# Weight requests, context products and bias products moved in a fused two-block Transformer kernel

## The reference

```
# first block: 16 experts, 32 tokens each; w_gate, w_up: 16 x 1024 x 2048, w_down: 16 x 2048 x 1024
hid = silu(xs @ w_gate) * (xs @ w_up);  eo = hid @ w_down
x = x + zeros.at[idx].add(gates * eo);  x = rms_norm(x, final_g)
# second block: context keys and values, from ctx alone
hc = modulate(rmsnorm(ctx, g_pre_mix), sh1c, sc1c)
kv_c = hc @ w_in[:, 1024:3072]          # keys 1024 columns, values 1024 columns
# second block: input projection; modulate adds the row sh1, so its product sh1 @ w_in is a bias row
h = modulate(rmsnorm(x, g_pre_mix), sh1, sc1)      # h * (1 + sc1) + sh1
q, k, v, z, gl = split(h @ w_in)                   # 7 parts of 1024 columns
```

## Time and profile before

| | us |
|---|---|
| median of 2 runs | 2217.85 (2216.74 to 2218.97) |
| the profiled execution, its own time | 2217.74 |
| its span, first to last instruction | 2215.9 |
| mean granted TensorE clock | 0.801 |
| PE busy | 1514.1 (68%) |
| DVE busy | 742.5 (34%) |
| DMA, mean over the span | 361 GB/s, 800.89 MB |

### The profile page before, as it was taken

How to read it: one execution, slowest core, us unless ns; L and a number is a source line. 1 busy time by engine, 2 the same in 40 slices (tenths; PEclk the granted TensorE clock), 3 DMA queues, 4 the chain that set the end, 5 groups by cost and what they waited for, 6 DMA issues and landing times.

```text
span 2215.9 us, 24722 instructions
## 1 busy us (share of the span) xinstructions
PE 1514.1 (68%) x10356; PEld 613.8 (28%) x10356; DVE 742.5 (34%) x1862; ACT 429.9 (19%) x998; POOL 309.4 (14%) x290
## 2 busy tenths in 40 slices
PE   9998676776565655659855988897686854434445
PEld 7554133221111111113211334454333620100001
DVE  5831100000000000000000235445767686776774
ACT  1430100000000000000000106443414542221222
POOL 0110000000000000000000000001343445444351
PEclk9999888877777777889977999898686975565555
DMA  9699989999999999999455824357999999999997
GB/s 408 269 423 383 421 348 399 402 392 428 427 429 428 428 428 427 428 420 425 197 232 232 335 88 176 114 190 293 382 418 416 421 420 420 421 421 420 421 420 308
DMA packets 76750, 800.89 MB, mean 361 GB/s; under 512 B 9088, under 2 KB 9216, under 8 KB 10592
## 3 DMA queue, kind: packets, MB, share of 16 engines
q1 hardware_dynamic: 39008, 530.66, 57.4%
q0 software_dynamic: 37632, 268.65, 29.3%
HBM read 798.03 MB, written 1.05 MB: 361 GB/s over the span
## 4 chain that ended last, share of the span: by engine, by line
DMA 42%; PE 42%; DVE 9%; ACT 3%; issue 2%; POOL 0%; SPq 0%; DVEq 0%; another core or an unknown queue 0%; ACTq 0%; POOLq 0%
DMA AR<-in_peer_uv,AR 13%; DMA AR<-in_w_up 12%; DMA AR<-in_w_down 10%; PE PS L413 5%; DMA AR<-in_w_gate 5%; PE PS L699 5%; PE PS L860 5%; PE PS L772 5%; PE PS L424 4%; PE PS L738 4%; DVE AR L1638 3%; PE PS L996 3%; PE PS L953 2%; PE PS L535 1%; PE PS L781 1%
## 5 line engine op out<-in xcount | busy, mean ns | idle before, releaser
L699 PE MATMUL PS<-AR 128*32 128x512 f32 x2048 | 330.1, 782 | 202.9 <-DMA AR<-in_w_up 129.3
L2072 POOL DMA_INDIRECT AR<-in_peer_uv,AR x256 | 293.6, 1147 | 1071.8 <-DVE AR L1629 772.7
L996 PE MATMUL PS<-AR 32*32 32x512 f32 x4032 | 224.7, 907 | 288.5 <-ACT AR L2008 285.2
L1638 DVE CUSTOM_DVE_ANT_0 AR<-AR 128x1024 f32<-128x1024 f32 x256 | 309.2, 1222 | 158.8 <-DMA AR<-in_peer_uv,AR 158.2
L738 PE MATMUL PS<-AR 128*32 128x512 f32 x1024 | 177.9, 756 | 131.4 <-DMA AR<-in_w_down 130.8
L1292 DVE TENSOR_TENSOR AR<-AR,PS 128x512 f32<-128x512 f32 x16 | 11.0, 687 | 593.4 <-PE PS L699 593.4
L699 PEld LDWEIGHTS PS<-AR 128*32 128x32 f32 x2048 | 64.7, 127 | 447.0 <-DMA AR<-in_w_up 208.8
L996 PEld LDWEIGHTS PS<-AR 32*32 32x32 f32 x4032 | 39.1, 124 | 428.8 <-ACT AR L2008 415.2
L413 PE MATMUL PS<-AR 128*128 128x512 f32 x288 | 136.1, 629 | 7.3 <-ACT AR L1704 4.0
L1320 DVE COPY AR<-PS 128x512 f32<-128x512 f32 x8 | 5.5, 692 | 315.8 <-PE PS L738 315.8
L860 PE MATMUL PS<-AR 128*128 128x512 f32 x224 | 106.4, 630 | 0.1
(11 more groups left out here) (312 smaller groups left out, 1441.6 us busy)
## 6 DMA issues: line engine op xcount, KB each, us to landing
AR<-in_w_up SPq DMA_DIRECT2D x64, 2048.0 KB, 20.8
AR<-in_w_down SPq DMA_DIRECT2D x64, 2048.0 KB, 15.9
AR<-in_w_gate SPq DMA_DIRECT2D x63, 2048.0 KB, 21.1
AR<-in_w_in SPq DMA_DIRECT2D x15, 2048.0 KB, 10.4
AR<-in_w_ada SPq DMA_DIRECT2D x12, 2048.0 KB, 12.8
AR<-in_w_in SPq DMA_DIRECT2D x14, 1024.0 KB, 12.7
AR<-in_w_out SPq DMA_DIRECT2D x6, 2048.0 KB, 8.0
AR<-in_peer_w_query SPq DMA_DIRECT2D x5, 2048.0 KB, 7.6
```

The lines of the kernel that those rows point to most:

```text
L699: x = pe.matmul(PS[32 * q:32 * q + 32, bk, :], XS[e][:, j, :], src[:, q * 512:(q + 1) * 512], start=(j == 0), stop=(j == 7), skip_group_ch ...
L996: x = pe.matmul(PS[c:c + 32, ACC[a][g], :], DI[t, p, r, :], AR[t, off + 1024 + m * 512:off + 1536 + m * 512], start=(h == 0 and p == 0), s ...
L1638: v.tensor_tensor_reduce(rows, rows, HB[:, a, :], 1.0, 0.0, MULT, ADD, DOT[:, ix, k:k + 1]).then_inc(*w.hit("dot", ix, k))
L2072: pool.indirect_dma_start(out=AR[:, off:off + 2048], out_offset=None, in_=D["peer_uv_2"], in_offset=bass.IndirectOffsetOnAxis(ap=EI[:, ix, ...
```

## The change

Four things. (1) The context weights no longer go through the ring: each has place `P6` to itself in turn and is asked for behind the up blocks of experts 4, 5, 6, 7; `P6` joins the ring only from the up half of expert 9. (2) PE multiplies each in four pieces (8 or 4 matmuls, 16 or 8 records), one after each gate chunk of experts 5 to 8. ACT copies the first half out ahead of that expert's `silu`, the second behind it. (3) Early blocks 6 to 13 are asked for before down block 2k + 2 and no longer before 2k (one pair of down blocks later); blocks 0 to 5 as before. (4) The four bias products of an early block go to four column groups (g = j) in place of two (g = 2n + j % 2), on rows 2r + n; `PAIRSUM` is made by DVE copies from `same32`, and `msk`, its memsets on POOL and DVE's wait for it go.

```
-            def context_keys(n, e):
-                features(("kc", n, e), ("ctx_k", n), HCT, e, [("turned", "hc", a, 1) for a in range(2)], e == 2)
-            def context_values(n, a):
-                tokens(("vc", n, a), ("ctx_v", n), HCT, a, [("turned", "hc", a, 1) for a in range(2)], a == 1)
+            def context_piece(i, c):
+                f = c // 2
+                group = ("kc", i, 2 * f) if i < 2 else ("vc", i - 2, f)
+                key = ("ctx_k", i) if i < 2 else ("ctx_v", i - 2)
+                if c % 2 == 0:
+                    b, before = banks.use(*group)
+                    w.wait_ge(*before)
+                b = banks.at(*group)
+                w.wait_ge("in", *key)
...
+                if i < 2:
+                    for j in range(8):
+                        x = pe.matmul(PS[:, b, c % 2 * 256:(c % 2 + 1) * 256], IN[key][:, j, c * 128:(c + 1) * 128], HCT[:, j, :],
+                                      start=(j == 0), stop=(j == 7))
+                else:
+                    for j in range(c % 2 * 4, c % 2 * 4 + 4):
+                        x = pe.matmul(PS[:, b, :], HCT[:, j, f * 128:(f + 1) * 128], IN[key][:, j, :], start=(j == 0), stop=(j == 7),
+                                      skip_group_check=True)
+                if c % 2:
+                    x.then_inc(*w.hit("mm", *group, also=[("used", *key)] if f else ()))
...
-                        if (name, c) == ("gate", 1):
-                            if e in (4, 5):
-                                context_keys(e - 4, 2)
-                            elif e in (6, 7):
-                                context_values(e - 6, 1)
+                        if name == "gate" and 5 <= e < 9:
+                            context_piece(e - 5, c)
...
-                elif e in (3, 4):
-                    context_keys(e - 3, 0)
-                elif e in (5, 6):
-                    context_values(e - 5, 0)
...
+                    r = 2 * r + n
                     for j in range(4):
-                        g = 2 * n + j % 2
-                        pe.matmul(PS[32 * g:32 * g + 32, BB, :], SHZ[:, j, 31 - r:63 - r], IN[key][:, j, :], start=(m == AHEAD[0][0] and j < 2),
-                                  stop=(m == AHEAD[-1][0] and j > 1), skip_group_check=True)
+                        pe.matmul(PS[32 * j:32 * j + 32, BB, :], SHZ[:, j, 31 - r:63 - r], IN[key][:, j, :], start=((m, n) == AHEAD[0]),
+                                  stop=((m, n) == AHEAD[-1]), skip_group_check=True)
...
-            w.wait_ge("msk")
             for g in range(4):
-                v.tensor_scalar(PAIRSUM[:, 32 * g:32 * g + 32], pk("same32"), msk[:, g // 2:g // 2 + 1], None, MULT).then_inc(
+                v.tensor_copy(PAIRSUM[:, 32 * g:32 * g + 32].rearrange("p (u r) -> p u r", u=2),
+                              pk("same32")[:, g // 2::2].unsqueeze(1).broadcast_to([128, 2, 16])).then_inc(
...
-            w.wait_ge("x1", 0, 1, 1)
-            w.step(pool.memset(msk, 0.0))
-            w.wait_step()
-            w.step(pool.memset(msk[0:64, 0:1], 1.0))
-            pool.memset(msk[64:128, 1:2], 1.0).then_inc(*w.hit("msk"))
...
-                        if (e, key, c) == (4, "upw", 0):
-                            w.wait_ge("mm", "xsa", 7)
+                        if (e, key, c) == (9, "upw", 0):
                             turn[0], ids[0] = 4, [*ids[0][turn[0] % 4:], *ids[0][:turn[0] % 4], P6]
                         ring((key, e, c), columns(key, e, c), 2, 2048)
...
-                elif e in (3, 4):
-                    square(("ctx_k", e - 3), "w_kv_2", e - 3)
-                elif e in (5, 6):
-                    square(("ctx_v", e - 5), "w_kv_2", e - 3)
+                elif 4 <= e < 8:
+                    if e == 4:
+                        w.wait_ge("mm", "xsa", 7)
+                    load(P6, ("ctx_k", e - 4) if e < 6 else ("ctx_v", e - 6), weight("w_kv_2", e - 4), 8, 512)
...
-                    if d % 2 == 0 and d // 2 < len(AHEAD):
-                        early(d // 2, (SA0, SA1, S50, S51, SA0, SA1)[d // 2] if d < 12 else (S50, S51)[d // 2 % 2])
+                    if d % 2 == 0 and d < 12:
+                        early(d // 2, (SA0, SA1, S50, S51, SA0, SA1)[d // 2])
+                    elif d % 2 == 0 and 14 <= d < 2 * len(AHEAD) + 2:
+                        early(d // 2 - 1, (S50, S51)[(d // 2 - 1) % 2])
                     down(1, i, blk)
```

More of the change, by code:

```diff
@@ L662, in context_turned @@
                     turn("scaled", "hc", CX[:, a, :], False, a, ("cx", a))
-            def context_keys(n, e):
-                features(("kc", n, e), ("ctx_k", n), HCT, e, [("turned", "hc", a, 1) for a in range(2)], e == 2)
-            def context_values(n, a):
-                tokens(("vc", n, a), ("ctx_v", n), HCT, a, [("turned", "hc", a, 1) for a in range(2)], a == 1)
+            def context_piece(i, c):
[7 more added lines that the diff above has]
+                w.wait_ge("in", *key)
+                w.wait_ge("turned", "hc", 0, 1)
+                w.wait_ge("turned", "hc", 1, 1)
+                if i < 2:
[8 more added lines that the diff above has]
+                    x.then_inc(*w.hit("mm", *group, also=[("used", *key)] if f else ()))
             picks(0, 0, 4)
@@ L1820, in scalar @@
             for e in range(16):
[L1821 to L1824, removed]
+                if e in (5, 6):
+                    context_key(e - 5, 0)
+                elif e in (7, 8):
+                    context_value(e - 7, 0)
                 w.wait_ge("mm", "gate", e, 3)
@@ L1828, in scalar @@
                 act.activation(SG, PS[:, BG, :], ACT.Silu).then_inc(*w.hit("silu", e))
+                if e in (5, 6):
+                    context_key(e - 5, 2)
+                elif e in (7, 8):
+                    context_value(e - 7, 1)
                 if e < 4:
@@ L1843, in scalar @@
                     root("cx", ssx)
-                elif e in (3, 4):
-                    context_key(e - 3, 0)
-                elif e in (5, 6):
-                    context_value(e - 5, 0)
             def junk(dc, a, gained):
```

## The result

The changed kernel takes 2118.12 us (median of 2 runs, 2116.07 to 2120.18) against 2217.85: ratio 0.955, 95% interval 0.9505 to 0.9595. Run again beside its parts it took 2113.04 (4 runs), ratio 0.953 (0.9506 to 0.9553). The forecast was 2114.

A forecast was written before the change was run, and what follows sets the result against it. Transfers bound the streaming part, except where context work held ring places and SP's waits let transfers run dry in the down stage. 2217.74 - 80.8 (down stage) - 22.5 (context) = 2114.4, said as 2114 us; range 2103 to 2140.

The forecast's parts named there:

- the drain: Down blocks 16 to 27: SP's wait lets transfers run dry; later early-block requests and faster bias products give 75.3 us.
- Bias products: Early blocks in the down stage: four column groups take 0.93 us in place of 1.70, saving 0.77 us each.
- Context: Stretch 305 to 480 us: own place and pieces raise 373 GB/s to 428, gaining the whole 22.5 us.
- Part 4: Removal of msk, three POOL memsets and a wait: up to 1 us either way, 0 taken.
- Changes of tiling: Context pieces among gate blocks: 16 more changes between 128-column and 32-column work on PE, priced at 0.
- B: Down stage: transfer starts not hidden, 2.5 us holes at bound requests, 15 to 20 us less gain, 2129 to 2134; chance 0.13.
- C: Context stretch: all pieces at 1.2 GHz, 11.4 us lost per expert, 2159; chance 0.05.
- D: Down stage: SP's wait stays last in the line, only 33 us gained, 2184; chance 0.04.
- E: Down stage: short PE waits put the clock to 1.2 GHz for good, slower at 2285; chance 0.02.
- The sum: Whole kernel: 2217.74 less 80.8 for the down stage and 22.5 for context work, 2114.4 us.

The follow-up runs named there:

- by twos: The changed kernel with the context pieces two by two, behind gate chunks 1 and 3 of the same experts: 2116.55 us, ratio 0.9538.

## Why the prediction was right, point by point

**What bounds, and the drain.** Right. The silent SP was named as the cause, and moving the requests alone gave 70.1 us against 70 worked out. The stretch from block 2 to block 29 takes 173.9 us against 173.7; inside it, pairs of 11.83 us in place of 11.91 and waits of 1.5 us offset each other.

**Bias products.** 1.00 + 1.72 us in place of 3.56 is 0.84 a pair, forecast 0.77. The part alone shortened its stretch by 9.4 us, forecast 10.8; beside the moved requests it was 10.3 and 11.6. The part's median is 14.3, and the 2 to 5 us beyond the stretch have no explanation that a run here shows.

**Context.** The mechanism is right: the stretch of 305 to 480 us runs at 428 GB/s. The term was 22.5, the profiled execution of the change gave 19.4, two others 22.2 and 21.5 (first early product at 970.12 and 970.84 against 992.30). Of the shortfall, 2.2 us lie before the changed code (the hidden rows of expert 2 are turned at 265.55 us, 263.37 before). From there on the profiled execution gains 21.5 us, and all the profiles of the table above give 19.0 to 21.6. So the term was up to 3 us too large in its own stretch as well, and the context part's median, 20.5, says the same. The changed kernel (first) and its second profiled execution (second), at 170 to 180 us:

```profile
170.00:180.00 10.00, 10.00 (x53) 5.19 (x52) 1.65 (x4) 0.00 (x0) 0.00 (x0) 0.83 1.01 426
```
```profile
170.00:180.00 10.00, 9.41 (x64) 5.57 (x60) 1.73 (x4) 0.00 (x0) 0.00 (x0) 1.00 1.01 426
```

At clock 0.83 PE gets through 53 records, at 1.00 through 64. The hidden rows of expert 2 are turned at 265.55 in the first and 263.02 in the second. The kernel with only the requests moved, the same as before up to there, has 0.83 as well (265.39), so this isn't the change's doing. With the POOL memsets kept it is 1.00 before and with the context part alone and 0.83 in that one, and without them also both, so they don't set it. Part 4's value of nothing was not tested by itself.

**Changes of tiling.** The prediction read its row as no cost, against the Trainium skill (TensorEngine Tiling (Array Packing), Key Properties: a change of tiling mode drains the TensorE). The row alone couldn't tell. The same two gate blocks and two context pieces of expert 6 can be read in two orders, in turns in the changed kernel (first) and by twos (second), PE busy throughout and, but for the block and piece behind the wait, at the same pace (line 715 is a gate or up block, 677 a piece):

```profile
391.79 3.64 PE L715 MATMUL PS<-AR 128*32 128x512 f32 x16 [4.73 <-DMA AR<-in_w_gate]
395.37 3.91 PE L677 MATMUL PS<-AR 128*128 128x256 f32 x16
399.21 1.93 PE L715 MATMUL PS<-AR 128*32 128x512 f32 x16
401.06 3.72 PE L677 MATMUL PS<-AR 128*128 128x256 f32 x16
404.71 1.92 PE L715 MATMUL PS<-AR 128*32 128x512 f32 x16
...
415.72 3.64 PE L715 MATMUL PS<-AR 128*32 128x512 f32 x32
```
```profile
408.46 3.64 PE L715 MATMUL PS<-AR 128*32 128x512 f32 x32
412.03 7.17 PE L677 MATMUL PS<-AR 128*128 128x256 f32 x32
419.13 3.64 PE L715 MATMUL PS<-AR 128*32 128x512 f32 x32
```

In turns they take 415.72 - 404.71 = 11.01 us, by twos 419.13 - 408.46 = 10.67. Two further changes of tiling cost 0.34 us, 0.17 each. That agrees with the skill in kind; whether it is the drain, the rows don't say. The price of 0 was wrong, and, as the prediction says, it didn't move the sum: the stream ran at 428 GB/s all the same.

**Rivals.** B was there at a tenth of its price. The stream in blocks 16 to 27 runs at 404 GB/s, 426 with the request one block later, so the requests do come a little late for it, but PE waits 1.5 us in all and not 15 to 20. C: the first gate block of an expert runs at the lower level (3.64 us in the rows above, after a wait of 4.73), its piece takes 3.91 us, so most of it is at the upper one, where the next takes 3.72. From the second chunk on a gate block with its piece takes 5.5 us, and there is no hole. D: SP's longest wait in the stretch is 11.3 us and was 24.7. E: the clock in blocks 16 to 27 is 1.00; after waits of 0.35 to 0.75 us the next block still takes 1.92 us.

The Trainium skill (DMA: Bandwidth & Descriptors, Anatomy of one DMA — SWDGE (gpsimd) path) gives its fixed part of about 2 us for transfers that GpSimd issues; the prediction leaves that out, and these are issued by SP. The dry requests show 0.37 + 9.46 us less 7.35 us of bytes, 2.5 us with the issue, for a 1 MB and a 2 MB block.

**The sum.** 2114 beside 2118 and 2113 measured is closer than its terms. By the parts alone the context part gave 2.0 us less than its term (20.5 against 22.5), the bias part 3.5 us more (14.3 against 10.8), and the two errors offset each other in part. That is luck. The drain, at 70 us by far the largest term, was right by itself.

## What to carry to other kernels

A wait in front of a request costs by what is in flight behind it: look in the issuing queue's list for the wait whose event needs the last thing asked for, and move that request behind others until the line in flight covers what the waited-for engine still has to do. Here two blocks (12.25 us with the small one) were enough and one cost 26 us. A block that is held longer than its neighbours doesn't belong in their ring; give it a place of its own before cutting the work on it into pieces, and check that the ring still runs at the full rate without that place.

## What was not expected of the hardware

The code behind the down stage takes 966 to 975 us in the profiled executions of kernels in which it is the same, so single profiles differ by up to 9 us at their end. And the granted clock at 170 to 180 us is 1.00 in some executions and 0.83 in others of the same code, worth 2.5 us here (265.55 against 263.02). Both are more than most small terms of the sum. A change between 128-column and 32-column work cost PE 0.17 us, which shows only where the same work is seen in two orders.
